# The second half of the vb product, the scores' row tiles and the low parts in the neighbourhood attention of a two-block kernel

## The reference

```python
proj = rms_norm(h, g_mix) @ w_in                 # -> qa, ka, va, qb, kb, vb, each 512 wide
oa = diff_attention(qa, ka, va, ...)             # 4 heads of 128
ob = neighbourhood_attention(qb, kb, vb, ...)    # 16 heads of 32; tokens as 8 rows x 64 columns
h = h + concatenate([oa, ob]) @ w_out
h = h + hier_moe(rms_norm(h, g_ffn), ...)        # 32 experts, 2 per token
h = h + rms_norm(p @ w_ple, g_ple) * sigmoid(rms_norm(h, g_plg) @ w_plg)
```

## Time and profile before

| | |
|---|---|
| median of 3 runs | 1560.24 us (1559.31 to 1563.29) |
| the profiled execution | 1559.29 us |
| its span in the trace | 1557.3 us |
| granted TensorE clock, share of full speed | 0.999 |
| busy share of the span: TensorE, its weight loads, VectorE, ScalarE, GpSimd | 97%, 68%, 45%, 34%, 11% |

### The profile page before, as it was taken

How to read it: one execution, slowest core, us unless ns; L and a number is a source line. 1 busy time by engine, 2 the same in 40 slices (tenths; PEclk the granted TensorE clock), 3 DMA queues, 4 the chain that set the end, 5 groups by cost and what they waited for, 6 DMA issues and landing times.

```text
span 1557.3 us, 19596 instructions
## 1 busy us (share of the span) xinstructions
PE 1517.0 (97%) x7812; PEld 1063.1 (68%) x7812; DVE 708.2 (45%) x1162; ACT 528.3 (34%) x907; POOL 167.5 (11%) x174
## 2 busy tenths in 40 slices
PE   6999999999999999999999989999999999999998
PEld 6776788888888888888877767754444444444366
DVE  5335332465444444468666788541122132132174
ACT  5234422354332423345355587421100011010042
POOL 1024100002111111110400210020000000000000
PEclk9999999999999999999999999999999999999999
DMA  8121422312222223222101132789999999999951
GB/s 332 45 72 62 189 94 95 122 66 87 105 108 90 100 82 108 108 95 82 54 30 53 68 150 76 307 342 391 421 420 421 421 421 421 420 422 420 421 231 55
DMA packets 45612, 311.73 MB, mean 200 GB/s; under 512 B 5184, under 2 KB 5696, under 8 KB 10192
## 3 DMA queue, kind: packets, MB, share of 16 engines
q1 hardware_dynamic: 42480, 296.74, 47.9%
q0 software_dynamic: 3040, 13.72, 2.4%
HBM read 302.05 MB, written 8.39 MB: 199 GB/s over the span
## 4 chain that ended last, share of the span: by engine, by line
PE 91%; DVE 4%; ACT 2%; issue 1%; DMA 1%; SPq 0%; DVEq 0%; ACTq 0%
PE bank L803 21%; PE bank L2532 14%; PE bank L2548 7%; PE bank L1465 7%; PE bank L838 7%; PE bank L855 4%; PE bank L2515 4%; PE bank L2565 4%; PE bank L2724 3%; PE bank L1322 3%; PE bank L816 2%; PE bank L826 2%; PE bank L873 1%; PE bank L847 1%; PE bank L864 1%
## 5 line engine op out<-in xcount | busy, mean ns | idle before, releaser
L627 DVE TENSOR_TENSOR w_lo<-M,w_hi 128x2048 fp32r<-128x2048 f32 x73 | 169.0, 2321 | 181.0 <-ACT w_hi L622 181.0
L2532 PE MATMUL bank<-M 128*64 128x512 f32 x1024 | 226.6, 595 | 1.0 <-ACT M L2620 1.0
L622 ACT ACTIVATE w_hi<-M 128x2048 fp32r<-128x2048 f32 x73 | 139.1, 1912 | 144.7 <-PE bank L803 56.9
L803 PE MATMUL bank<-HTL,w_hi 128*128 128x512 f32 x432 | 168.1, 389 | 0.0
L803 PE MATMUL bank<-HTH,w_lo 128*128 128x512 f32 x432 | 168.1, 389 | 0.0
L803 PE MATMUL bank<-HTH,w_hi 128*128 128x512 f32 x432 | 168.1, 389 | 0.0
L2532 PEld LDWEIGHTS bank<-M 128*64 128x64 f32 x1024 | 71.9, 137 | 134.7 <-issue 133.7
L2548 PE MATMUL bank<-M 128*64 128x512 f32 x512 | 113.6, 595 | 1.5 <-DMA M<-in_w 1.5
L2686 DVE TENSOR_TENSOR X<-bank,X 128x512 f32<-128x512 f32 x69 | 46.5, 688 | 109.7 <-PE bank L2565 109.6
L803 PEld LDWEIGHTS bank<-HTH,w_lo 128*128 128x128 f32 x432 | 81.1, 188 | 16.9
L803 PEld LDWEIGHTS bank<-HTH,w_hi 128*128 128x128 f32 x432 | 81.1, 188 | 16.8
(11 more groups left out here) (376 smaller groups left out, 2820.4 us busy)
## 6 DMA issues: line engine op xcount, KB each, us to landing
M<-in_w SPq DMA_DIRECT2D x192, 1024.0 KB, 11.2
M<-in_wd SPq DMA_DIRECT2D x78, 1024.0 KB, 4.8
M<-in_nb SPq DMA_DIRECT2D x4, 1536.0 KB, 7.3
X<-in_x SPq DMA_DIRECT2D x4, 512.0 KB, 7.4
M<-in_tb POOLq DMA_DIRECT2D x8, 256.0 KB, 4.6
M<-in_rows POOLq DMA_DIRECT2D x4, 512.0 KB, 6.5
rowb<-in_rows POOLq DMA_DIRECT2D x4, 512.0 KB, 6.1
xs_parts<-XSH POOLq DMA_DIRECT2D x1, 2048.0 KB, 10.4
```

The lines of the kernel that those rows point to most:

```text
L622: e.activation(hi[:, :], slots[slot_of[n]], ACT.Copy).then_inc(split_hi_done, 1)
L627: e.tensor_tensor(lo[:, :], slots[slot_of[n]], hi[:, :], ALU.subtract).then_inc(split_lo_done, 1)
L803: m = e.matmul(out[:, :], w[:, k0 + k, n0:n0 + 128], v[k], start=(k == 0 and i == 0), stop=(k == len(hi) - 1 and i == 2))
L2532: m = e.matmul(b[64 * s:64 * s + 64, :], Xe[:, 4 * kh + k, o + C * s:o + C * s + C], unit_w(key, 4)[:, k, :], start=(kh == 0 and k == 0), ...
```

## The change

Eight edits go together.

1. Of the 24 woven halves only 20 stay in the differential steps, one a step from step 8 on (none in step 12, two in 13). The four halves of vb 2 and 3 go into neighbourhood steps 0 to 3 (`VB_AT`); VectorE and ScalarE empty them in neighbourhood steps 2 and 4.
2. Unit in2 11 is split in differential step 13, not 11.
3. QM and all work of GpSimd in these stages go. ScalarE writes qbT in the order that the blocks need, and a score matmul takes 32 rows of qbT; each head's scores have a bank.
4. The values are turned by group and half (`vj_pe`), in steps 0, 1, 6 and 9 (half of the turns ahead, half at the step's end), all copied by ScalarE, into bank 4 from step 6 on.
5. "oa" 2 and 3 are turned in steps 4 and 5, both in bank 4; oa is held elsewhere than in HTH and HTL for heads 0 and 1.
6. "o2a" is in steps 7 to 17 (`O2A_IN`), seven of eight in bank 4. "no" has bank 6 alone.
7. `O2_SPLIT`: high and low part both in steps 3, 9, 14, 16.
8. The first bias table has its own place and is loaded earlier. This place holds pT, and the spare slot is now used by the stage: so the ple unit and pT are loaded a second time after the stage, the ple unit as the first of `expert_loads`, which now waits for the stage's end.

```diff
-        woven_by = [min(len(WOVEN), (3 * i + 4) // 2) for i in range(len(DIF) + 3)]
+        woven_by = [min(len(WOVEN), (3 * i + 4) // 2, i + 5 - (i == 12)) for i in range(len(DIF) + 3)]
...
-        SPLIT_AT = {5: 6, 8: 7, 11: 8}
+        SPLIT_AT = {5: 6, 8: 7, 13: 8}
...
-        OA_AT = {0: 2, 2: 3}
-        VJ_AT = {0: range(0, 4), 1: range(4, 8)}
-        O2A_IN = ((4, 5), (6, 7), (8, 9), (11, 12), (14, 15), (16, 16), (17, 17), (18, 18))
+        OA_AT = {4: 2, 5: 3}
+        VJ_EARLY, VJ_LATE = {0: (0, 0), 1: (1, 0), 6: (2, 0), 9: (3, 0)}, {0: (0, 1), 1: (1, 1), 6: (2, 1), 9: (3, 1)}
+        VB_AT = {0: (2, 0), 1: (2, 1), 2: (3, 0), 3: (3, 1)}
+        O2A_IN = ((7, 7), (8, 8), (10, 10), (11, 12), (13, 13), (14, 15), (16, 16), (17, 17))
...
+                    ps.put(("nt", i - 2, half), [(7, {2: 6, 3: 4}.get(i, 5))[half]])
+            if i >= 3 and (i - 3) % 4 == 0:
+                ps.put(("no", (i - 3) // 4), [6], counted=False)
...
-        open_slots = deque([(SPARE_SLOT, "free")] + ...
+        open_slots = deque([(SPARE_SLOT, "nbr")] + ...
...
+            if G == 2:
+                for r in range(2):
+                    a = e.activation(qbT.rearrange("p k (j r c) -> p k j r c", j=4, c=16)[:, :, :, 2 * t + r, :],
+                                     b[:, :].rearrange("p (k r j c) -> p k r j c", k=4, r=2, c=16)[:, :, r, :, :], ACT.Copy, scale=scale)
...
-            both = [claim(e, ("ns", i, hp)) for hp in range(2)]
-            for s in range(2):
-                for hp, (b, fills) in enumerate(both):
-                    half = slice(64 * hp, 64 * hp + 64)
-                    m = e.matmul(b[:, s * 256:s * 256 + 256], QM[hg % 2][half, 2 * hp + s, 128 * j:128 * j + 128],
-                                 k4[half, hg, :, KB[j]:KB[j] + 32], start=True, stop=True)
+            for hh in range(4):
+                b, fills = claim(e, ("ns", i, hh))
+                at = slice(32 * hh, 32 * hh + 32)
+                e.matmul(b[:, 0:256], qbT[at, hg, 128 * j:128 * j + 128], k4[at, hg, :, KB[j]:KB[j] + 32], start=True,
+                         stop=True).then_inc(fills, 1)
...
+        def vj_pe(e, f, q):
+            taken(e, ("vb", f))
+            b, fills = claim(e, ("vj", f, q))
+            for n in range(4):
+                v = 4 * q + n
+                m = e.transpose(b[:, n * 128:(n + 1) * 128], vbJ[f][:, v // 2, v % 2 * 128:(v % 2 + 1) * 128], ident)
+            m.then_inc(fills, 1)
...
-        O2_SPLIT = {2: 0, 12: 2, 15: 1, 16: 3}
+        O2_SPLIT = {3: 0, 9: 2, 14: 1, 16: 3}
...
             for i in range(len(NBR) + 3):
+                if i == 4:
+                    vb_act(e, ("vb", 3))
                 if i < len(NBR):
                     nbr_exp_act(e, i)
...
-                if i - 1 in O2_SPLIT:
-                    split_dve(e, unit["out2", O2_SPLIT[i - 1]])
-                if i in O2A_SUM:
-                    out2_add(e, "o2a", *O2A_SUM[i])
+                if i in OA_AT:
+                    oa_lo_dve(e, OA_AT[i])
+                if i in O2_SPLIT:
+                    split_low(e, unit["out2", O2_SPLIT[i]])
                 if i >= 3 and NBR[i - 3][1] == 3:
                     hg = NBR[i - 3][0]
...
+            for k in range(2):
+                e.dma_start(pT[k], pT_d[:, k, :]).then_inc(d_pT, 16)
...
-            for n in range(NDENSE + 1, len(keys)):
+            for n in range(NDENSE, len(keys)):
```

More of the change, by code:

```diff
@@ L632, in next_split_act, with next_split_low @@
             split_act(e, unit[key] + NSPLIT)
-        def next_split_dve(e, key):
-            split_dve(e, unit[key] + NSPLIT)
+        def next_split_low(e, key):
+            split_low(e, unit[key] + NSPLIT)
         def split_ready(e, key):
@@ L862, in gemm_rows_part @@
             for k in range(4):
-                for i, src in enumerate((HTH,) if low else (HTH, HTL)):
-                    m = e.matmul(out[:, :], src[:, k, t * 128:(t + 1) * 128], w[:, k, :], start=(low == k == i == 0),
+                for i, src in enumerate((OAH,) if low else (OAH, OAL)):
+                    m = e.matmul(out[:, :], src[k][:, t * 128:(t + 1) * 128], w[:, k, :], start=(low == k == i == 0),
                                  stop=(low == 1 and k == 3))
@@ L1775, in vb_parts @@
             for j in range(4):
-                yield vbJ[:, key[1], j, :].rearrange("p (r c) -> p r c", c=32), b4[:, :, KB[j]:KB[j] + 32], j == 3, empties
+                yield vbJ[key[1]][:, j, :].rearrange("p (r c) -> p r c", c=32), b4[:, :, KB[j]:KB[j] + 32], j == 3, empties
         def vb_act(e, key):
@@ L1816, in build @@
         E2 = [mem(2 * UNIT + 1536 + 512 * i, 512) for i in range(3)]
-        QM = [region(2048 * i, 4, 512) for i in range(2)]
-        NB = [mem(SPL[2], 4, 3, 256), mem(2 * UNIT, 4, 3, 256)]
+        NB = [region(13376, 4, 3, 256), mem(2 * UNIT, 4, 3, 256)]
         lam = stat(6)
@@ L2102, in nbr_pe @@
                     hg, j = NBR[i - 3]
-                    if i == 3:
-                        for v in range(8):
-                            taken(e, ("vj", v))
                     if j == 0:
+                        for q in range(2):
+                            taken(e, ("vj", hg, q))
                         claim(e, ("no", hg))
@@ L2153, in nbr_act @@
                                      ACT.Copy).then_inc(empties, 1)
+                if i in VJ_LATE and i >= 2:
+                    vj_act(e, *VJ_LATE[i])
                 if i in O2_SPLIT:
-                    filled(e, {2: ("vj", 7), 12: ("ns", 11, 1), 15: ("o2a", 3, 0), 16: ("ns", 11, 1)}[i])
-                    if i >= 12:
-                        for hp in range(2):
-                            taken(e, ("ns", 11, hp))
+                    filled(e, {3: ("vj", 1, 1), 9: ("vb", 3), 14: ("o2a", 3, 0), 16: ("vj", 3, 1)}[i])
                     if i == 16:
-                        e.wait_ge(q_spread, 16)
+                        for hh in range(4):
+                            filled(e, ("ns", len(NBR) - 1, hh))
                     split_act(e, unit["out2", O2_SPLIT[i]])
@@ L2180, in nbr_dve @@
                     nbr_score_dve(e, i)
-                for v in VJ_DVE.get(i, ()):
-                    evac_dve(e, Vj[:, v, :], ("vj", v))
                 if i == 2:
-                    oa_lo_dve(e, OA_AT[0])
+                    vb_dve(e, ("vb", 2))
+                if i in O2A_SUM:
+                    out2_add(e, "o2a", *O2A_SUM[i])
                 if 1 <= i <= len(NBR):
@@ L2278, in expert_loads @@
                     filled(e, ("o2", 3, 1))
-                elif before == "free":
-                    pass
                 elif before < NDENSE:
@@ L2575, in ple_pe @@
         def ple_pe(e, t, h):
+            early = (t, h) in PL_AT.values()
             if (t, h) == PL_AT[11]:
+                e.wait_ge(d_w_early, 16)
+                e.wait_ge(d_pT, 48)
+            if t == h == 0:
                 unit_ready(e, unit["ple", 0])
-                e.wait_ge(d_pT, 48)
+                e.wait_ge(d_pT, 80)
             w = unit_w(("ple", 0), 2)
@@ L2824, in end_dve @@
             dve_own.mark(e.reciprocal(r, sq))
-            split_dve(e, unit["plg", 3])
+            split_low(e, unit["plg", 3])
             e.wait_ge(dve_own.sem, dve_own.n)
```

203 lines of the change are left out of this document (94 added, 109 removed).

## The result

The changed kernel takes 1568.39 us, median of 5 runs (1567.42 to 1570.19), against 1560.24 of the kernel before on the same chip: ratio 1.0052, 95% interval 1.0041 to 1.0063. It is slower by 8.15 us where 5.8 were forecast; the time lies in the range. The profiled execution took 1569.1 us with a span of 1567.2, that is 9.8 and 9.9 us more than before.

What follows compares the result with a forecast made beforehand. TensorE, busy 97% of the span, was taken as the bound, with VectorE and ScalarE nearly as full in the neighbourhood. Terms 0 - 6.9 + 3.0 + 10.0 + 0.3 = +6.4 us gave 1565.7, stated as 1566, range 1556 to 1573.

Steps and rivals of the forecast that it cites:

- vb halves at 0: Four vb halves move from differential steps to neighbourhood steps 0 to 3: 11.5 us leave and 11.5 enter, sum 0.
- differential end +3.0: Differential steps 13 to 16: TensorE idles 3.4 us for VectorE's weights behind unit 11's low part, 0.4 before; net of GpSimd +3.0.
- Score blocks -6.9: Neighbourhood scores: four 32-row matmuls, each in its own bank, save 0.43 us a block, 16 blocks, -6.9 us.
- The third rival: Score blocks: row tiles don't overlap four ways, 6.9 us not saved, some 2.5 of it in holes: 1570 us; chance 0.13.
- GpSimd out: Masked copies disappear, VectorE's scaling returns from 1.00 to 0.49 us; worth 0.8 us, counted in the differential chain.
- Holes +10.0: Neighbourhood steps: TensorE's holes come to 16.2 us against 6.2 before, +10.0 us; none in steps 0 to 3.
- the 'no' accumulators have one bank in place of two: Neighbourhood steps 15 and 16: group 3's first product waits for group 2's low half, hole 4.1 us, then 1.4.
- Transfers +0.3: Expert loads: 5 us of lost lead and 1.6 MB more fall into the 8 us of silence; taken as +0.3 us.
- One sign named for being wrong: Expert stage: the prediction would be wrong if TensorE waits for DMA there.
- The sum: Whole kernel: all terms together +6.4 us on the profiled execution's 1559.29, giving 1565.7; chance 0.48.
- half the holes: Neighbourhood holes: blocks slip into holes that the prediction kept apart, +6.4 - 6: 1560 us; chance 0.18.
- the case's own range: Whole kernel: 1561 to 1570 us for the prediction's own sum, before widening to 1556 and 1573.

Runs made afterwards that it cites:

- experiment 6: Changed kernel with unit 11's high part in differential step 13 made ahead of ScalarE's square root and vb 0's copies: 1564.44 us, ratio to before 1.0026.
- experiment 5: Changed kernel with the low part of weight unit 11 back in differential step 11 in place of 13: 1573.20 us, ratio to before 1.0072.
- experiment 7: Changed kernel with score matmuls of 64 rows, two at a time, in place of 32-row tiles: 1571.11 us, ratio to before 1.0066.
- Experiment 2: Changed kernel with VectorE, in step 14, emptying group 2's low half from the accumulators before making unit 1's low part: 1567.53 us, ratio to before 1.0047.
- experiment 3: Changed kernel with output unit 1's low part alone made a step later, in step 15 in place of 14: 1561.52 us, ratio to before 0.9999.
- experiment 4: Kernel before, two accumulator banks kept, with output units' low parts made in the same step as their high parts: 1574.61 us, ratio to before 1.0086.
- experiment 8: Changed kernel without the second load of the per-layer-embedding unit, first expert unit thereby issued earlier: 1567.97 us, ratio to before 1.0041.

## Why the prediction was right, and where not

- *vb halves at 0, differential end +3.0*: the total is right, 8.8 us earlier for 8.5; its parts are not, and the match is luck. The mechanism, VectorE late behind unit 11's low part, is there, and experiment 6 shows it. But idle grew by 1.0 only, not by 3.0: the new holes are 2.34 and 0.61 us, and three of before are gone, 0.43, 0.37 and 1.05. The last, in front of the score block at 844.78, stood behind the same low part in step 11; the prediction took the cost at the new place and not what the old one gave back. The other 1.7 us are the lower clock. Experiment 6 won hole and clock together, 4.0. Moving the low part back (experiment 5) costs more; the loss is the order within step 13, not the step.
- *Score blocks -6.9*: right, 0.65 us for 1.07, and 6.3 of busy time in experiment 7. This was the estimate of parallel loads as in TensorEngine Tiling (Array Packing), section Tiling Modes, of the Trainium skill. The Trainium skill's rule in TensorE: Matmul & The Clock Gate, section LDWEIGHTS, read as eight loads in series, would have given 0.85; the measurement decides against that reading. As a price of the edit by itself 6.9 would be wrong: undone, it costs 2.7. The third rival, which has these tiles not overlap, is out; of its 2.5 us in holes experiment 7 shows 2.1.
- *GpSimd out*: as said. VectorE's scaling took 0.49 us again (877.91), for 1.00 beside GpSimd's work.
- *Holes +10.0*: +6.3, and this was the term mis-sized. Steps 0 to 3 had none, as said. Steps 4, 5, 6 and 9 had theirs at the rows forecast, 1.39 for 1.6 at vb 3's bank, 1.80 at head 3's turn for 2.2, 1.13 and 1.35 at the value turns for 1.0 and 1.3; step 15 had 4.30 for 4.1. Too much was counted at the scores behind unit 0's low part (0.34 for 1.1), at the values' turn in the same bank (none for 1.1), in step 11 behind unit 2's low part (none for 1.0) and at the product behind step 15 (0.83 for 1.4).
- *The cause of step 15*: wrong in the step "the 'no' accumulators have one bank in place of two". The size fitted, the reason was half of it. Experiment 2 frees the bank in time and wins 0.9; experiment 3 leaves the one bank and wins 6.9; experiment 4 has two banks and loses 14. What costs is a low part in the step of its high part, with anything that TensorE needs behind it on VectorE's queue.
- *The clock*: missing altogether. All rows of before stood at 1.00, and I priced every block at full clock. Three stretches near half clock cost about 6.4 us in the neighbourhood, as much as the added idle, 6.3; a fourth ahead of it cost 1.7. That the profile of before shows no fall in these stages is no reason to expect none when holes of 2 to 4 us are added. The Trainium skill warns of it, TensorE: Matmul & The Clock Gate, section HAM oscillation: a gap in TensorE's work slows the work that follows. The trace agrees for the hole of 4.30 us; behind that of 2.34 the work was slow here and not in experiment 3.
- *Transfers +0.3*: +1.4 in the profile, cause open (experiment 8). Loads began at the stage's end and without silence, as forecast. One sign named for being wrong did show in a small way: TensorE waits 0.8 us for expert units in the first kind of their products, where before it waited for none.
- *The sum*: +9.9 for +6.4. It is -6.9 for the blocks, +7.3 of idle where 13.0 was forecast, +8.1 of lower clock where nothing was, and +1.4 for the expert stage. By its idle alone the change would have come near the rival "half the holes", 1560; the clock, which no part of the prediction had, brought the time back into the case's own range. That the time was met is so in good part luck.

## What to carry to other kernels

When one engine makes the first part of a pair and another the second, count what stands behind the second in its queue, not only who reads it; a step of distance between the two parts cost nothing here and its absence 7 us, at one place alone. When such a wait moves to another step, count also the hole that goes at the old place. A saving on the busiest engine is worth its full price only where that engine has no holes. After a hole of several us, price what follows at the lower clock too, and look for a fall in the granted clock wherever a variant idles more than before.

## What the runs showed of the hardware

- Four matmuls of 32 rows in four banks, each with its own weights, ran at 0.65 us a block for 1.07 of the 64-row form, and up to eight matmul instructions were in flight in one 50 ns slice, where before had four:

```profile
884.85:884.90 0.05, 0.05 (x8) 1.00 0.00 0
```

- The granted clock fell from 1.00 to 0.50 in a hole of TensorE or within 0.7 us of its end: with idles of 2.34, 4.30 and 4.85 us, with short ones in a row (1.39, 0.34 and 1.80 us, 907 to 912; 1.35 and 0.18, 936 to 938), and in experiment 4 behind one of 1.98. It came back after 3 to 10 us. The fall is not bound to the code. The kernel of experiment 3 has the same hole of 2.34 us, at 877.79, and stays at 1.00, and so it does from 938 to 942 us, where the changed kernel is at 0.52; the kernel before has idles of 0.81, 0.42, 1.98 and 0.45 us from 902 to 911 and stays at 1.00 too. The kernel of experiment 3, then the kernel before:

```profile
876.00:884.00 8.00, 4.60 (x40) 4.43 (x40) 5.13 (x15) 6.43 (x13) 0.00 (x0) 1.00 0.00 0
...
938.00:942.00 4.00, 3.82 (x25) 3.11 (x21) 2.09 (x1) 1.88 (x2) 0.00 (x0) 1.00 0.00 0
```
```profile
902.00:912.00 10.00, 6.34 (x61) 4.82 (x60) 9.83 (x30) 10.00 (x28) 3.38 (x4) 1.00 0.04 18
```

- The stage of the experts, from its first matmul on, took 529.4 to 532.4 us in the profiles of 14 kernels with the same expert code, with 0 to 2.0 us of waits for expert units in the first of its two kinds of products, and these times did not follow whether the per-layer-embedding unit was loaded again.
